# Two attention layers and three feed-forward blocks on one core: order of VectorE in the sparse attention, 14 tokens fewer in two projections, half-width level products

## Chip, cores and metric

The kernel runs on 1 core of one Trainium2 chip. The metric is the device time of one execution in microseconds; shown are the median and the extremes of 3 runs. "Profile" is one further execution, taken by the hardware profiler. A core has TensorE (PE in the rows; its weight loads are PEld), VectorE (DVE), ScalarE (ACT), GpSimd (POOL) and SyncE (SP).

## The reference, cut to what matters

One sequence of 512 tokens, 1024 wide, in float32, goes through two blocks. Three pieces concern the change.

```python
# first block: 16 meta tokens stand ahead of the 512 (528 tokens)
q_a, k_a, v_a, f_a, q_b, k_b, v_b, g_a, g_b = split(rms_norm(h) @ w_in)
mixed = (sigmoid(g_a) * y_a + sigmoid(g_b) * y_b) @ w_out
...
return h[:, N_META:]
# second block, gated linear attention (GLA, 4 heads of 128), per chunk of 64 tokens
decay = exp(where(causal, b[t] - b[s], -inf))     # b: cumulative sum of the log gates
scores = einsum('bhtd,bhsd,bhtsd->bhts', q, k, decay)
# second block, sparse attention (8 heads of 128, blocks of 128 queries)
_, sel = top_k(score, 128)                        # by an indexer
logits = q . kv_sel * dc ** -0.5 + bias           # masked where not selected
probs = softmax(logits)
out = probs @ kv_sel
```

After the first block's attention the kernel keeps only 514 of the 528 tokens: the convolution of width 3 that follows looks two tokens back, and the 16 meta tokens are dropped at the end.

## The kernel before, in words

**The whole.** Activations lie transposed in SBUF (features on the partitions, tokens along the free dimension). Every weight is streamed once from HBM in units of 128x2048 (`raw`); ScalarE rounds a unit to a short float (`whi`, cast at L718, or in quarters at L730), GpSimd subtracts for the rest (`wlo`, L655), and TensorE makes three products for each tile: `whi` by the activations' high part, `whi` by their low part, `wlo` by their high part (`tile_products`, L2197). The order of work on each engine is written out by hand, engine by engine, and semaphores tie the engines together; nothing is scheduled by a planner.

**Projections of the first block.** A chunk is 128 output features by 528 tokens, 8 input tiles of 3 products, each in two pieces of 256 and 272 tokens (`wide_places`): 48 matmuls. The second queries (`q_b`, 4 chunks), second keys (4 chunks) and gates (16 chunks) are interleaved with the attention steps by `dense`. VectorE takes a finished chunk out of PSUM times the inverse root (`scaled`, L1511, L1513). The gates go through a sigmoid on ScalarE (L951) and VectorE reads 514 of their tokens (L1721, L1722). `SKIP` is 14. The corner queries (`corner_queries`) read tokens 512 to 527 of the second queries.

**GLA.** For each head there are 9 kinds of item (`GI`), 36 items in all: kind 0 is the diagonal product, kinds 1 to 7 are levels, kind 8 is what crosses the four 128-token tiles. At level L a tile of 128 tokens is cut into groups of 2^L; the product between the first and the second half of a group is needed. VectorE subtracts (`gf` at L1982, L1983), ScalarE exponentiates, VectorE multiplies (L1992, L1993), TensorE multiplies each 128-token tile of `gf` by itself (L2845, 128 columns for each of 4 tiles, in plain float32, two passes each, so that 8 matmuls stand in the profile), and VectorE copies under a mask of bytes into `sd` (L2016, 512 elements). TensorE fills in with tiles of a projection (`gr_tiles`, L2197).

**Sparse attention.** 32 items, of (block, head): 16 that alternate between blocks 3 and 0 (512 and 128 keys wide), then 16 that alternate between blocks 2 and 1 (384 and 256). Item n goes this way:

- TensorE: scores into a bank (L2929), plus the mask (L2930).
- VectorE: adds the bias and takes the minimum in one instruction (the "minimum", L2087, into `dl`; the logits have their sign turned).
- ScalarE: exponential with the sum (L1294).
- VectorE: reciprocal of the sum and scaling (L2094, L2096, the "normalisation").
- TensorE: transposes into PSUM (L2945).
- ScalarE: copies out (`dpt`, L1290).
- TensorE: the product with the values (L2955).
- ScalarE: high part (`x2hi`, L1283). VectorE: low part (`x2lo`, L2103).

In step n of their loops TensorE does scores n, transposes n-2 and value product n-3; ScalarE does the high part n-4, copy n-2 and exponential n; VectorE does minimum n, normalisation n-1 and low part n-4. TensorE waits for the normalisation (`da_norm`) before the transposes, and for the low part two items back (`da_lo`) before the value product. In steps 8 to 11 ScalarE also casts a quarter of a weight unit (L730).

Of the kernel before, what the change touches and what calls it, by code (L numbers as in the profile page):

```python
# [27 lines left out]
ALU = mybir.AluOpType  # L28
# [3 lines left out]
P = 128  # L32
# [167 lines left out]
def build(nc, wstream, h0, fw, cvec, alpha_w, rel_bias, p2, ident_c, masks_c, gmask_c, onehot_c, out):  # L200
    n_units = wstream.shape[0]
    with ExitStack() as ctx:
# [214 lines left out]

        def diag_seen(q):

            return sum(1 for x in range(q + 1) if GI[x][1] < 8)  # L420
# [49 lines left out]
        U_LAST += [T_GATES + 2 * KC * (i + 1) for i in range(8)]  # L470

# [237 lines left out]
        def _(act):  # L709
# [235 lines left out]
            for m in range(8):  # L945
                if m % 2 == 1:
                    hi_of(U_O + m // 2 + 2)
                if m == 0:
                    act.wait_ge(sig("evac"), D_END)
                for c in (m, 8 + m):  # L950
                    nc.scalar.activation(gates[:, c, :], gates[:, c, :], ACT.Sigmoid).then_inc(sig("gate_on"), 1)  # L951
                act.wait_ge(sig("y_sum"), m + 1)
                nc.scalar.copy(yhi[:, m, :], yt[2 * (m % 2)][:]).then_inc(sig("y_hi"), 1)
# [416 lines left out]
        def _(dve):  # L1370
# [133 lines left out]
            def wide(d):  # L1504

                return regions[:, STAGE1[d][0] // 2, LO:LO + T1]

            def scaled(d, dst, scale=None):

                if scale is None:  # L1510
                    vec.tensor_tensor(dst, wide(d), rt[:], ALU.mult).then_inc(sig("evac"), 1)  # L1511
                else:
                    vec.scalar_tensor_tensor(out=dst, in0=wide(d), scalar=scale, in1=rt[:], op0=ALU.mult,  # L1513
                                             op1=ALU.mult).then_inc(sig("evac"), 1)
# [63 lines left out]
            scaled(7, qkf[:, 6, :])  # L1578
            dve.wait_ge(sig("unit_done"), 4)
# [388 lines left out]
            def halves(ap, L):  # L1968
                v = ap.rearrange("p (n c) -> p n c", c=2 ** L)
                return v[:, :, 0:2 ** (L - 1)], v[:, :, 2 ** (L - 1):]  # L1970

            for q in range(NG + 2):
# [30 lines left out]
                if 0 <= m < NG:  # L2003
# [8 lines left out]
                    elif kind < 8:  # L2012
                        dve.wait_ge(sig("g_cp"), diag_seen(m) - 1)
                        mk = ga_m[:, (kind - 1) * P:kind * P] if kind < 5 else gb_m[:, (kind - 5) * P:(kind - 4) * P]
                        mk = mk.rearrange("p (a c) -> p a c", a=1).to_broadcast([P, 4, P])
                        vec.copy_predicated(sd[hd % 2][:], mk, src).then_inc(sig("g_cp"), 1)  # L2016
# [63 lines left out]
            for n in range(ND + 4):  # L2080
                if n < ND:
                    j, hd = DI[n]
                    w = P * (j + 1)
                    dve.wait_ge(sig("da_s"), n + 1)
                    if n >= 3:
                        dve.wait_ge(sig("da_t"), n - 2)
                    vec.tensor_tensor_reduce(dl[n % 3][:, 0:w], bank(n % 4)[:, 0:w], bias[:, hd, w - 1::-1], 1.0, 3e38,  # L2087
                                             ALU.add, ALU.min, dst_[:, 0, n:n + 1]).then_inc(sig("da_max"), 1)
# [10 lines left out]
                if 0 <= m < ND:  # L2099
# [4 lines left out]
                                      ALU.subtract).then_inc(sig("da_lo"), 1)  # L2104

# [82 lines left out]
        def _(pe):  # L2188
# [65 lines left out]
            def chunk_tile(u, c, k, banks):  # L2254

                return tile_products(u % 2, 2 * k + c, wide_places(banks), lambda tok: xhi[:, k, tok],
                                     lambda tok: xlo[:, k, tok], k == 0, k == KC - 1)
# [88 lines left out]
            def dense(first, last):  # L2346

                for t in range(first, last):
# [10 lines left out]
                    ins = chunk_tile(u, c % 2, k, STAGE1[d])  # L2359
# [462 lines left out]
            for q in range(1, NG + 4):  # L2822
# [9 lines left out]
                if 0 <= m < NG:  # L2832
# [3 lines left out]
                    if kind < 8:  # L2836
                        if m >= 3 and (seen := diag_seen(m - 3)):
                            pe.wait_ge(sig("g_cp"), seen)
                        for j in range(4):
# [3 lines left out]
                            else:  # L2843
                                left = right = gf[m % 3][:, tile]
                            ins = mm(bank(m % 3)[:, tile], left, right, start=True, stop=True)  # L2845
# [230 lines left out]
```

## Time and profile before

| what | value |
|---|---|
| median of 3 runs | 2203.33 us (2202.96 to 2203.38) |
| time of the profiled execution | 2203.01 us |
| its span, first to last instruction | 2201.1 us |
| TensorE busy | 2159.8 us (98%) |
| VectorE, ScalarE, GpSimd busy | 992.3, 753.4, 1005.0 us |
| mean granted TensorE clock | 0.997 |
| DMA, mean over the span | 89 GB/s |

Busy times of TensorE come from modelled ends, and consecutive matmuls overlap in them; the distance from one start to the next says more than a duration. A bracket in a row gives the idle time of the engine before it and what ended it.

### The profile page before, as it was taken

The numbers are of one execution on the slowest core, as the hardware profiler recorded it, in microseconds if no ns is written. First come the engines' busy times: TensorE is split into PE (matmuls) and PEld (weight loads), VectorE is DVE, ScalarE is ACT, GpSimd is POOL, SyncE is SP. The second block draws the span as 40 slices with busy tenths as digits, with TensorE's granted clock in tenths as the row PEclk, the third lists the DMA queues.
The fourth block names the chain that finished last, engine by engine and source line by source line (L and its number), as shares of the span: only waits on it lengthen the run. The fifth ranks groups of instructions, "written<-read, shape, count | busy, mean of one in ns | idle before, by whom it ended". The sixth has DMA issues, their size and how long they took to land.

```text
span 2201.1 us, 31220 instructions
## 1 busy us (share of the span) xinstructions
PE 2159.8 (98%) x12448; PEld 1856.6 (84%) x12448; DVE 992.3 (45%) x1447; ACT 753.4 (34%) x1003; POOL 1005.0 (46%) x812
## 2 busy tenths in 40 slices
PE   8999999989999999999999999999999999999998
PEld 7897999989999887888888787878777888888886
DVE  5144454279888208322201619661875452322017
ACT  4133454343222216322213324551336332222134
POOL 4322223455555547555544543254331555555444
PEclk9999999999999999999999999999999999999999
DMA  4321111212222223222222321024220223222222
GB/s 163 101 72 64 58 59 59 97 58 96 95 94 82 111 100 111 104 95 95 95 99 93 103 93 59 22 75 140 90 77 20 85 90 112 90 101 95 96 97 95
DMA packets 31837, 194.94 MB, mean 89 GB/s; under 512 B 3968, under 2 KB 4480, under 8 KB 9984
## 3 DMA queue, kind: packets, MB, share of 16 engines
q1 hardware_dynamic: 26352, 182.66, 23.3%
q10 hardware_dynamic: 5392, 10.95, 1.6%
q8 instruction: 68, 1.11, 0.2%
q14 instruction: 25, 0.20, 0.0%
HBM read 189.24 MB, written 4.23 MB: 88 GB/s over the span
## 4 chain that ended last, share of the span: by engine, by line
PE 81%; issue 7%; DVE 5%; POOL 4%; ACT 1%; DMA 0%; SPq 0%; DVEq 0%; POOLq 0%; ACTq 0%
PE ps L2197 71%; POOL wlo L655 4%; PE ps L2747 2%; DVE sqa L1428 1%; PE ps L2955 1%; PE ps L2872 1%; PE ps L2929 1%; DVE x2lo L1416 1%; PE ps L2845 1%; ACT whi L718 1%; PE ps L2476 0%; PE ps L2499 0%; PE ps L2910 0%; PE ps L2535 0%; DVE sd L2016 0%
## 5 line engine op out<-in xcount | busy, mean ns | idle before, releaser
L655 POOL TENSOR_TENSOR wlo<-raw,whi 128x512 fp32r<-128x512 f32 (+2 forms) x808 | 1004.7, 1276 | 1172.9 <-ACT whi L718 1081.5
L718 ACT CAST whi<-raw 128x2048 fp32r<-128x2048 f32 x165 | 315.3, 1911 | 825.2 <-PE ps L2197 767.4
L2197 PE MATMUL ps<-x2hi,whi 128*128 128x512 f32 x1136 | 450.8, 397 | 1.3 <-DVE x2lo L1416 1.1
L2197 PE MATMUL ps<-x2hi,wlo 128*128 128x512 f32 x1136 | 442.9, 390 | 0.0
L2197 PE MATMUL ps<-x2lo,whi 128*128 128x512 f32 x1136 | 442.8, 390 | 0.0
L2197 PE MATMUL ps<-xhi,whi 128*128 128x256 f32 x1344 | 276.6, 287 | 20.7 <-DVE xlo L1481 9.5
L2197 PE MATMUL ps<-xlo,whi 128*128 128x256 f32 x1344 | 273.6, 285 | 0.0
L2197 PE MATMUL ps<-xhi,wlo 128*128 128x256 f32 x1344 | 273.4, 285 | 0.0
L2197 PEld LDWEIGHTS ps<-x2hi,whi 128*128 128x128 f32 x1136 | 213.7, 188 | 50.5 <-issue 7.1
L2197 PEld LDWEIGHTS ps<-x2lo,whi 128*128 128x128 f32 x1136 | 213.8, 188 | 45.3 <-issue 2.6
L2197 PEld LDWEIGHTS ps<-x2hi,wlo 128*128 128x128 f32 x1136 | 213.6, 188 | 44.7
L2197 PEld LDWEIGHTS ps<-xhi,whi 128*128 128x128 f32 x1344 | 210.9, 191 | 22.7 <-POOL wlo L655 13.5
L2197 PEld LDWEIGHTS ps<-xlo,whi 128*128 128x128 f32 x1344 | 211.0, 191 | 0.0
L2197 PEld LDWEIGHTS ps<-xhi,wlo 128*128 128x128 f32 x1344 | 210.9, 191 | 0.0
L2197 PE MATMUL ps<-hhi,whi 128*128 (+1 forms) x528 | 205.4, 389 | 0.0
L2197 PE MATMUL ps<-hlo,whi 128*128 (+1 forms) x528 | 205.4, 389 | 0.0
L2197 PE MATMUL ps<-hhi,wlo 128*128 (+1 forms) x528 | 205.4, 389 | 0.0
L2197 PEld LDWEIGHTS ps<-hhi,whi 128*128 128x128 f32 x528 | 99.1, 188 | 20.6
L2197 PEld LDWEIGHTS ps<-hhi,wlo 128*128 128x128 f32 x528 | 99.1, 188 | 20.6
L2197 PEld LDWEIGHTS ps<-hlo,whi 128*128 128x128 f32 x528 | 99.1, 188 | 20.4
L1440 DVE TENSOR_TENSOR cvl<-ps,fold 128x1024 f32<-128x1024 f32 x22 | 26.9, 1224 | 189.3 <-PE ps L2197 189.3
L1878 DVE SCALAR_TENSOR_TENSOR h<-ps,h 128x512 f32<-128x512 f32 x16 | 10.9, 681 | 209.7 <-PE ps L2197 209.7
(439 smaller groups left out, 2747.4 us busy)
## 6 DMA issues: line engine op xcount, KB each, us to landing
raw<-wstream SPq DMA_DIRECT2D x170, 1024.0 KB, 4.8
h<-h SPq DMA_DIRECT2D x4, 528.0 KB, 8.5
ncb<-c_rows ACTq DMA_DIRECT2D x8, 256.0 KB, 3.4
ple_rows<-ple_out ACTq DMA_DIRECT2D x4, 512.0 KB, 3.9
bias<-bias_rows ACTq DMA_DIRECT2D x8, 256.0 KB, 4.6
ple<-ple_rows ACTq DMA_DIRECT2D x4, 512.0 KB, 5.6
out_dram<-outb SPq DMA_DIRECT2D x8, 256.0 KB, 2.9
raw<-wstream ACTq DMA_DIRECT2D x4, 256.0 KB, 7.2
```

What stands on the lines that cost most here:

```text
L655: return nc.gpsimd.tensor_tensor(wlo[b][:, cols], raw[b][:, cols], whi[b][:, cols].bitcast(F32), ALU.subtract)
L718: nc.scalar.copy(whi[b][:], raw[b][:]).then_inc(sig("hi_done"), 1)
L1416: vec.scalar_tensor_tensor(out=xl[:, k, 0:T], in0=view(k), scalar=cv[:, gain + k:gain + k + 1], in1=xh[:, k, 0:T].bitcast(F32), op0=ALU.mu ...
L1428: vec.tensor_tensor(squared[:, 0, :], squared[:, 0, :], squared[:, k, :], ALU.add).then_inc(sig("sq_added"), 1)
L1440: return vec.tensor_tensor(dst, pair(src), scale, ALU.mult)
L1878: vec.scalar_tensor_tensor(out=hview(m), in0=bank(m), scalar=0.5, in1=hview(m), op0=ALU.mult, op1=ALU.add).then_inc(sig("down_evac"), 1)
L2197: ins = mm(dst, w[slot][:, cols], xx(tok), start=first and p_ == 0, stop=last and p_ == 2, skip_group_check=True)
L2747: ins = mm(gv_bank(half, j), xx[:, k if first else k + 4, tok], ww[u % 2][:, cols], start=(first and k == 0 and p_ == 0), stop=(not first ...
L2845: ins = mm(bank(m % 3)[:, tile], left, right, start=True, stop=True)
L2872: ins = mm(dst[:, t_ * P:(t_ + 1) * P], gvt[:, s_, vc], rhs, start=(x_ == 0), stop=(x_ == len(plan) - 1), skip_group_check=True)
L2929: mm(dst, dq[:, hd, j * P:(j + 1) * P], ckvf[:, 0:w], start=True, stop=False)
L2955: ins = mm(bank(6 + m % 2)[:, 0:P], ckvt[:, b, :], dpt[m % 2][:, b * P:(b + 1) * P], start=(b == 0), stop=(b == j))
```

## The change

Three parts.

1. **514 tokens.** The second queries' 4 chunks and the 16 gate chunks leave out the first 14 tokens: the pieces are 256 and 258 instead of 256 and 272 (`first_of`). VectorE's `scaled` and ScalarE's sigmoid work on 514. A `memset` on VectorE sets the second queries' first 14 tokens to zero.
2. **Level products' later halves.** For kinds 1 to 7 the moving operand is only the second half of each group: 64 columns for each tile instead of 128, written side by side in PSUM, and the masked copy covers 256 elements instead of 512, with strides on the mask and the destination.
3. **Order in the sparse attention.** In VectorE's step n the minimum n moves from the front of the step to its end, behind normalisation n-1 and low part n-4.

```diff
+        def halves(ap, L):
+            v = ap.rearrange("p (n c) -> p n c", c=2 ** L)
+            return v[:, :, 0:2 ** (L - 1)], v[:, :, 2 ** (L - 1):]
+
+        def late_of(m, kind):
+            late = bank(m % 3)[:, 0:4 * P // 2]
+            return late.rearrange("p (j n c) -> p j n c", j=4, c=2 ** (kind - 1))
...
+        def first_of(d):
+            return SKIP if D_QKB <= d < D_QKB + 4 or d >= D_GATES else 0
...
-                    nc.scalar.activation(gates[:, c, :], gates[:, c, :], ACT.Sigmoid).then_inc(sig("gate_on"), 1)
+                    used = gates[:, c, SKIP:T1]
+                    nc.scalar.activation(used, used, ACT.Sigmoid).then_inc(sig("gate_on"), 1)
...
             def scaled(d, dst, scale=None):
 
+                dst, roots_ = dst[:, first_of(d):], rt[:, first_of(d):]
...
+            step.up(vec.memset(qkb[:, 0:4, 0:SKIP], 0.0))
...
-                        mk = mk.rearrange("p (a c) -> p a c", a=1).to_broadcast([P, 4, P])
-                        vec.copy_predicated(sd[hd % 2][:], mk, src).then_inc(sig("g_cp"), 1)
+                        n, b = P >> kind, 2 ** (kind - 1)
+                        dst = sd[hd % 2][:].rearrange("p j (n c) -> p j n c", c=2 * b)[:, :, :, b:]
+                        mk = mk.rearrange("p (a n c) -> p a n c", a=1, c=2 * b)[:, :, :, b:].to_broadcast([P, 4, n, b])
+                        vec.copy_predicated(dst, mk, late_of(m, kind)).then_inc(sig("g_cp"), 1)
...
             for n in range(ND + 4):
-                if n < ND:
-                    j, hd = DI[n]
-                    w = P * (j + 1)
-                    dve.wait_ge(sig("da_s"), n + 1)
-                    if n >= 3:
-                        dve.wait_ge(sig("da_t"), n - 2)
-                    vec.tensor_tensor_reduce(dl[n % 3][:, 0:w], bank(n % 4)[:, 0:w], bias[:, hd, w - 1::-1], 1.0, 3e38,
-                                             ALU.add, ALU.min, dst_[:, 0, n:n + 1]).then_inc(sig("da_max"), 1)
                 m = n - 1
...
+                if n < ND:
+                    j, hd = DI[n]
+                    w = P * (j + 1)
+                    dve.wait_ge(sig("da_s"), n + 1)
+                    if n >= 3:
+                        dve.wait_ge(sig("da_t"), n - 2)
+                    vec.tensor_tensor_reduce(dl[n % 3][:, 0:w], bank(n % 4)[:, 0:w], bias[:, hd, w - 1::-1], 1.0, 3e38,
+                                             ALU.add, ALU.min, dst_[:, 0, n:n + 1]).then_inc(sig("da_max"), 1)
...
                 r, cut = regions[:, banks[0] // 2, :], first_token + HALF
                 return [(r[:, LO:BANK], slice(first_token, cut)), (r[:, BANK:BANK + T1 - cut], slice(cut, T1))]
...
-                    ins = chunk_tile(u, c % 2, k, STAGE1[d])
+                    ins = chunk_tile(u, c % 2, k, STAGE1[d], first_of(d))
...
-                                left = right = gf[m % 3][:, tile]
-                            ins = mm(bank(m % 3)[:, tile], left, right, start=True, stop=True)
+                                left, right = gf[m % 3][:, tile], halves(gf[m % 3][:, tile], kind)[1]
+                            dst = bank(m % 3)[:, tile] if kind == 0 else late_of(m, kind)[:, j]
+                            ins = mm(dst, left, right, start=True, stop=True)
```

VectorE's own order in the sparse attention, steady part of the wide and narrow items. ISA is the minimum (the second ISA row reads its result), RECIPROCAL and TENSOR_SCALAR are the normalisation, TENSOR_TENSOR is the low part; `dl_206` to `dl_208` are the three buffers of `dl`. Before:

```order
L2087 ISA dl_208,dst<-ps,bias 128x512 [waits da_t,da_s]
L2087 ISA dst 128x1
L2094 RECIPROCAL dst<-dst 128x1 [waits da_max,da_exp]
L2096 TENSOR_SCALAR dl_207<-dl_207,dst 128x128 [waits dve_step]
L2103 TENSOR_TENSOR x2lo<-ps,x2hi 128x128 [waits da_hi]
L2087 ISA dl_206,dst<-ps,bias 128x128 [waits da_t,da_s]
```

Each minimum is followed by the normalisation of the item before it, in another buffer. With the change:

```order
L2117 ISA dl_208,dst<-ps,bias 128x128 [waits da_t,da_s]
L2117 ISA dst 128x1
L2100 RECIPROCAL dst<-dst 128x1 [waits da_max,da_exp]
L2102 TENSOR_SCALAR dl_208<-dl_208,dst 128x128 [waits dve_step]
L2109 TENSOR_TENSOR x2lo<-ps,x2hi 128x128 [waits da_hi]
L2117 ISA dl_206,dst<-ps,bias 128x512 [waits da_t,da_s]
```

Each minimum is now followed by the normalisation of the same item, in the same buffer, and the next minimum stands behind that.

The level products on TensorE, in the first head of GLA. Before:

```order
L2845 MATMUL ps<-gqk 128x128 x4
L2845 MATMUL ps<-gf_179 128x128 x4
L2197 MATMUL ps<-x2hi,whi_51 128x512
```

With the change:

```order
L2860 MATMUL ps<-gqk 128x128 x4
L2860 MATMUL ps<-gf_179 128x64 x4
L2211 MATMUL ps<-x2hi,whi_51 128x512
```

The number of matmuls and their order stay; a level's matmuls have 64 columns.

## Rows read from the trace of the kernel before

**Rows 1.** Windows: length, busy us (count) by engine, clock; GLA, then sparse attention.

```profile
1343.60:1363.00 19.40, 17.23 (x114) 14.09 (x115) 18.88 (x43) 10.32 (x27) 10.04 (x16) 1.00 0.19 73
1667.52:1689.67 22.15, 22.13 (x147) 18.42 (x146) 16.12 (x71) 15.64 (x55) 0.44 (x1) 1.00 0.13 49
```

**Rows 2.** Timeline (start, duration), sparse attention, one pair of 512 and 128.

```profile
1649.96 0.69 DVE L2087 CUSTOM_DVE_ANT_0 dl<-ps,bias 128x512 f32<-128x512 f32 x1 [1.05 <-PE ps L2930]
...
1650.77 0.29 DVE L2096 TENSOR_SCALAR dl<-dl,dst 128x128 f32<-128x128 f32 x1
1650.88 0.72 ACT L1294 ACTIVATE dl<-dl,dst 128x512 f32<-128x512 f32 x1
1650.98 0.28 DVE L2103 TENSOR_TENSOR x2lo<-ps,x2hi 128x128 fp32r<-128x128 f32 x1
...
1651.11 0.33 PE L2945 MATMUL ps<-ident,dl 128*128 128x128 f32 x1 [0.24 <-DVE dl L2096]
1651.18 0.28 DVE L2087 CUSTOM_DVE_ANT_0 dl<-ps,bias 128x128 f32<-128x128 f32 x1
...
1651.51 0.19 ACT L1294 ACTIVATION_READ_ACCUMULATOR dl<-dl,dst 128x1 f32 x1
...
1651.73 0.16 DVE L2094 RECIPROCAL dst<-dst 128x1 f32<-128x1 f32 x1 [0.27 <-ACT dl L1294]
...
1651.90 0.42 ACT L1294 ACTIVATE dl<-dl,dst 128x128 f32<-128x128 f32 x1
1651.93 0.48 DVE L2096 TENSOR_SCALAR dl<-dl,dst 128x512 f32<-128x512 f32 x1
...
1652.33 0.28 DVE L2103 TENSOR_TENSOR x2lo<-ps,x2hi 128x128 fp32r<-128x128 f32 x1
...
1653.66 0.69 DVE L2087 CUSTOM_DVE_ANT_0 dl<-ps,bias 128x512 f32<-128x512 f32 x1 [1.05 <-PE ps L2930]
```

**Rows 3.** Timeline, sparse attention, the first minimum and its exponential.

```profile
1635.96 0.69 DVE L2087 CUSTOM_DVE_ANT_0 dl<-ps,bias 128x512 f32<-128x512 f32 x1 [2.75 <-PE ps L2930]
...
1636.75 0.73 ACT L1294 ACTIVATE dl<-dl,dst 128x512 f32<-128x512 f32 x1
```

**Rows 4.** Timeline, sparse attention, a weight cast on ScalarE; minimum and exponential of 384.

```profile
1655.30 0.61 ACT L730 CAST whi<-raw 128x512 fp32r<-128x512 f32 x1
...
1681.26 0.56 DVE L2087 CUSTOM_DVE_ANT_0 dl<-ps,bias 128x384 f32<-128x384 f32 x1 [0.66 <-PE ps L2930]
...
1681.96 0.62 ACT L1294 ACTIVATE dl<-dl,dst 128x384 f32<-128x384 f32 x1
```

**Rows 5.** Timeline, sparse attention: third minimum; last reciprocal; next stage's first matmul.

```profile
1642.76 0.69 DVE L2087 CUSTOM_DVE_ANT_0 dl<-ps,bias 128x512 f32<-128x512 f32 x1 [3.02 <-PE ps L2930]
...
1693.16 0.16 DVE L2094 RECIPROCAL dst<-dst 128x1 f32<-128x1 f32 x1
...
1695.29 0.48 PE L2197 MATMUL ps<-x2hi,whi 128*128 128x512 f32 x1
```

**Rows 6.** Timeline of TensorE, GLA, first head, a level that waits and two matmuls ahead.

```profile
1350.70 0.39 PE L2197 MATMUL ps<-x2lo,whi 128*128 128x512 f32 x1
1350.93 0.40 PE L2197 MATMUL ps<-x2hi,wlo 128*128 128x512 f32 x1
1352.29 1.16 PE L2845 MATMUL ps<-gf 128*128 128x128 f32 x8 [0.96 <-DVE gf L1993]
```

**Rows 7.** Groups by line and shape, GLA, VectorE: count, busy us, mean ns.

```profile
L2016 DVE COPY_PREDICATED sd<-ga_m,ps 128x512 f32<-128x512 int8 x16 | 11.6, 724 | 10.3 <-PE ps L2845 10.3
L1982 DVE TENSOR_TENSOR gf<-nbt 128x256 f32<-128x256 f32 x24 | 10.0, 417 | 1.8 <-PE ps L2852 1.8
```

**Rows 8.** Timeline of TensorE, end of the program: plain float32 with one moving column.

```profile
2190.89 1.05 PE L3006 MATMUL ps<-per,sq 128*128 128x1 f32 x8
```

**Rows 9.** Chain that ended last: a gate chunk of 528; output projections of 514.

```profile
293.32 5.91 PE ps L2197 x48
...
358.89 89.89 PE ps L2197 x744
```

More of the change, by code:

```diff
@@ L1504, in wide @@
             def wide(d):
-                return regions[:, STAGE1[d][0] // 2, LO:LO + T1]
+                return regions[:, STAGE1[d][0] // 2, LO:LO + T1 - first_of(d)]
             def scaled(d, dst, scale=None):
+                dst, roots_ = dst[:, first_of(d):], rt[:, first_of(d):]
                 if scale is None:
-                    vec.tensor_tensor(dst, wide(d), rt[:], ALU.mult).then_inc(sig("evac"), 1)
+                    vec.tensor_tensor(dst, wide(d), roots_, ALU.mult).then_inc(sig("evac"), 1)
                 else:
-                    vec.scalar_tensor_tensor(out=dst, in0=wide(d), scalar=scale, in1=rt[:], op0=ALU.mult,
+                    vec.scalar_tensor_tensor(out=dst, in0=wide(d), scalar=scale, in1=roots_, op0=ALU.mult,
                                              op1=ALU.mult).then_inc(sig("evac"), 1)
@@ L1966, in _ @@
                               ).then_inc(sig("nb_ready"), 1)
-            def halves(ap, L):
-                v = ap.rearrange("p (n c) -> p n c", c=2 ** L)
-                return v[:, :, 0:2 ** (L - 1)], v[:, :, 2 ** (L - 1):]
             for q in range(NG + 2):
@@ L2252, in wide_places, with chunk_tile @@
                 return [(r[:, LO:BANK], slice(first_token, cut)), (r[:, BANK:BANK + T1 - cut], slice(cut, T1))]
-            def chunk_tile(u, c, k, banks):
-                return tile_products(u % 2, 2 * k + c, wide_places(banks), lambda tok: xhi[:, k, tok],
+            def chunk_tile(u, c, k, banks, first_token=0):
+                return tile_products(u % 2, 2 * k + c, wide_places(banks, first_token), lambda tok: xhi[:, k, tok],
                                      lambda tok: xlo[:, k, tok], k == 0, k == KC - 1)
```

## The prediction

> **What bounds the kernel now.** I read the page first: TensorE is busy for 98% of the span (the table above), so a change counts where TensorE works without a pause, or where it pauses for another engine. Then the windows of the two stages that the change touches. In the first head of GLA, VectorE is busy for 18.88 of 19.40 us and TensorE has pauses: VectorE sets the pace there. In the second half of the sparse attention (widths 384 and 256) TensorE is busy for 22.13 of 22.15 us [rows 1]. In the first half (512 and 128) a pair of items takes 3.70 us, from one wide minimum to the next; TensorE's transposes wait 0.24 us in each pair for a normalisation, while VectorE itself sits idle for 1.05 us ahead of the wide minimum [rows 2]. Projections run without pauses [rows 9].
>
> The sums below are made against the profiled execution, 2203.01 us with a span of 2201.1; the median of the runs is 0.3 us above it, and I add the sum to the median. A measurement of this kernel can tell about 0.2% (4.4 us) from no change; the chances use that bound.
>
> **514 tokens.** 20 chunks lose 14 columns in 24 of their 48 matmuls. A gate chunk of 528 takes 5.91 us for 48 matmuls, 123.1 ns each; the output projections of 514, part of which also start at token 14, take 89.89 us for 744, 120.8 ns each [rows 9]. That is 2.3 x 48 = 0.11 us in a chunk and 2.2 us in 20 chunks. TensorE sets the end there, so all of it counts. Bounds: 0 (a start at an odd place costs what the columns save) and 3.2 us (14 columns of 20 x 24 matmuls at 120.8 / 257 = 0.47 ns a column). I take 2.2. VectorE's shorter evacuations, the shorter sigmoids and the memset lie beside TensorE's work and count as nothing; if that cover were gone, the memset would cost under 0.2 us.
>
> **Level products.** 28 groups of eight matmuls go from 128 to 64 moving columns. Does the group get shorter? Eight plain float32 matmuls with a single moving column still take 1.05 us [rows 8], and eight with 128 columns 1.16 [rows 6]. The distance between them is thus not set by the columns, and I count nothing for seven of the eight. The last one's columns are not hidden behind another weight load: 64 columns fewer there are up to 0.05 us in a group, 28 x 0.05 = 1.4 us, of which I take 1.0, since some groups end in a wait on VectorE anyway.
>
> The masked copy covers 256 elements instead of 512. It takes 724 ns; a two-operand instruction of 256 elements takes 417 [rows 7]. I take 0.45 us for the new copy, 0.27 less. This counts only where TensorE waits for VectorE. At the level that waits longest, the start of the matmuls comes 1.36 us after that of the matmul ahead, where 0.23 is usual (1350.70 to 1350.93): 1.1 us lost [rows 6]. Two smaller losses of 0.2 and 0.3 lie before it in the same head. Three copies lie ahead of that point in a row of VectorE's instructions without idle time, so 0.8 us comes back there. In the other heads VectorE has idle time, and the loss that can come back is what one to three copies ahead of a wait give; from the starts I count five such places (0.3, 0.3, 0.5, 0.3, 0.3). Together 2.5 us. The waits at the change of head stay, because there VectorE waits for TensorE first. Bounds: 0 (strided copies no faster) and 4. The two terms of this part: 3.5 us, bounds 0 and 5.5.
>
> **The order in the sparse attention.** What it removes: the wide minimum no longer stands ahead of the narrow item's normalisation. What it adds is a wait: normalisation n-1 waits for exponential n-1 on ScalarE, which waits for minimum n-1, and now minimum n is queued behind it. Before, minimum n ran while ScalarE was at exponential n-1. Now VectorE has nothing to do meanwhile, and all items form one chain: minimum, exponential, reciprocal, scaling, low part, next minimum. Its length for one item of 512:
>
> - start of the minimum to start of the exponential: 0.79 us [rows 3];
> - exponential to the end of its sum's read: 1651.51 + 0.19 - 1650.88 = 0.82; to the reciprocal 0.03; to the scaling 0.20; to the low part 0.40 [rows 2];
> - low part to the next minimum: 1651.18 - 1650.98 = 0.20 [rows 2].
>
> Sum 2.44 us. For 128: minimum 0.28 and about 0.07 to the exponential, 0.42 + 0.10, 0.03, 0.20, 0.21, 0.20 [rows 2]: 1.5 us. A pair takes 3.9 us instead of 3.70. For 384 and 256: 0.56 + 0.10 + 0.62 + 0.10 + 0.03 + 0.20 + 0.32 + 0.20 = 2.1, and 0.43 + 0.05 + 0.52 + 0.10 + 0.03 + 0.20 + 0.27 + 0.20 = 1.8 [rows 4], with steps of the widths that have no row put between those that have: 3.9 us again. There TensorE now gets through a pair in about 3.15 us without a pause (22.15 us for seven pairs [rows 1]), so most of the loss lies in the half that has no waits today.
>
> The end: the third minimum starts at 1642.76, behind scores that side work of TensorE holds back in both orders [rows 5]. From there 30 items are 15 pairs, 58.5 us; the last reciprocal comes 0.7 us before their end (scaling, low part and a step), at 1642.8 + 57.8 = 1700.6 instead of 1693.16: 7.4 us later. ScalarE's four casts of 0.61 us [rows 4] stand between exponentials and now delay the high part for which the low part in the chain waits; by the same steps that is 0.1 us for a wide item and 0.3 for a narrow one, twice each: 0.8 us. Behind the last reciprocal TensorE has a value product less to do, 0.2 us. Sum: **8.0 us longer**. Bounds: 6.5 (the quarters hidden, steps 2% shorter) and 10.
>
> **Sum.** -2.2 - 3.5 + 8.0 = +2.3 us: 2203.33 + 2.3 = 2205.6 us, within 0.2%.
>
> **Rivals.**
>
> *The level halves give nothing, and the chain stands alone (slower).* The mechanism: a masked copy whose runs are 1, 2 or 4 elements goes at the pace of the words it passes over, not of those it copies, so that 256 strided elements cost what 512 did. For it: no row has a masked copy with a stride. Against it: the subtractions L1982 have the same strides and take 417 ns on average over the levels [rows 7]. Then the sum is -2.2 + 8.0 and, with the last matmul's 1.0, +4.8 us: 2208.1, over the bound. It decides from a new copy of about 0.65 us on. The Trainium skill (SBUF — State Buffer, "Door 1: The DMA port swizzle") says that each access that crosses to a new 16-byte line pays a penalty; by that rule level 1 would pass over as many lines as before and gain little, the levels from 3 on would gain in full. Chance 0.25.
>
> *The matmuls do get shorter.* If the distance went with the columns, each of 224 matmuls would save 0.055 us, 12 us in all; VectorE has 18.88 of 19.40 us of work in the first head, less 1.9 for seven copies, so at most half can show: another -6 us, 2199.6 us. Against it: the single-column matmuls [rows 8]. The Trainium skill (TensorE: Matmul & The Clock Gate, "Back-to-back issue gap") gives N / 2.4 + 2.5 ns for an isolated matmul, which is this rival's rule; by its "LDWEIGHTS" section, 107 ns for 128 weight columns, the distance would stay, and the one-column row agrees with the latter. Chance 0.1.
>
> *The new order helps (faster).* If the exponential were early enough, each wide pair would lose its pauses: 3.70 us with 0.24 in the row, at most 0.6 us with the wait for the low part behind it, times 7 pairs: 4 us saved instead of 8 lost, 2203.33 - 2.2 - 3.5 - 4 = 2193.6. For it: VectorE is idle for 1.05 us ahead of the wide minimum, and normalising the narrow item would fit in there. Against it: the narrow minimum pays for it, since it now stands behind the wide exponential (0.82 us), with a reciprocal that already waits 0.27 us for ScalarE today [rows 2]. Chance 0.08.
>
> **How the numbers follow.** The forecast case has 0.57, the rivals 0.25, 0.1 and 0.08. In the forecast case the bounds of the terms reach 4.4 us in about a quarter of it, and the slow rival crosses that bound in most of its chance: slower 0.3. Faster: the last rival and a little of the one before, 0.1. The rest, 0.6, is within 0.2%. Range: from 2199.0, which takes in the shorter matmuls, to 2211.5, which takes in the slow rival with the chain at its upper bound of 10 us (514 tokens -1, chain +10, level products -1); only the rival with the helpful order lies wholly outside.
>
> **What the profile of the changed kernel would show.** Right: gate chunks of 48 matmuls in 5.80 us; level groups as long as before; masked copies near 0.45 us; in the sparse attention VectorE idle ahead of every reciprocal until the exponential ends, a pair every 3.9 us in both halves, TensorE with pauses in the second half, and the next stage's first matmul 8 us later than the stage's start alone explains. Wrong: a pair of 384 and 256 still in 3.15 us, or VectorE's wait ahead of the minimum still for TensorE's mask product. A level group of eight in 0.6 us would make the second rival right, a masked copy of 0.65 us or more the first.

## The result, and the profile after

The changed kernel takes 2208.86 us (median of 9 executions, 2207.16 to 2216.11) against 2203.33 us before (2202.92 to 2204.18 in the same comparison). The ratio is 1.0031, with a 95% interval of 1.0023 to 1.0040: slower, by 5.5 us. That lies inside the range given (2199.0 to 2211.5), but the forecast was 2205.6 and its likeliest case "within 0.2%"; the interval lies wholly beyond 0.2%, an outcome to which the prediction gave 0.3.

| what | before | after |
|---|---|---|
| median | 2203.33 us | 2208.86 us |
| profiled execution | 2203.01 us | 2207.16 us |
| its span | 2201.1 us | 2205.3 us |
| TensorE busy | 2159.8 us | 2158.5 us |
| VectorE busy | 992.3 us | 987.3 us |
| mean granted clock, profile | 0.997 | 0.997 |
| mean granted clock, all executions | 0.994 to 0.997 (77 of the later comparisons) | 0.991 to 0.997 |

The profiled execution is the fastest of the nine, 4.15 us above that of before. The other eight reach up to 9 us higher, most of them at a lower mean clock. Both are looked at below.

**Where the 4.15 us come from.** I laid the two profiles side by side and followed the start of the same TensorE matmul in both:

| place (time in before) | after minus before |
|---|---|
| end of the first block's first projections, 380 | -2.4 us |
| a sum of squares in the feed-forward, 873 | -2.8 us |
| GLA, last head, 1414 | -5.6 us |
| end of the selection, 1618 | -4.3 us |
| third item of the sparse attention, 1642.8 | -4.2 us |
| first matmul behind it, 1695.29 | +3.4 us |
| a sum of squares near the end, 2156 | +4.1 us |
| end of the span | +4.2 us |

*Projections.* The chain of waits shows the gate chunk at 5.81 us, 0.10 less than in [rows 9]. In that chain a long stretch of the output projections stays at the old pace, 87.31 us for 726 matmuls, 120.3 ns each:

```profile
281.36 5.81 PE ps L2211 x48
...
358.93 87.31 PE ps L2211 x726
```

*GLA.* TensorE's timeline, first head, the groups that stand ahead of a projection tile:

```profile
1344.60 1.10 PE L2860 MATMUL ps<-gf 128*128 128x64 f32 x8
1345.51 0.48 PE L2211 MATMUL ps<-x2hi,whi 128*128 128x512 f32 x1
...
1347.94 0.40 PE L2211 MATMUL ps<-x2hi,wlo 128*128 128x512 f32 x1
1348.18 1.09 PE L2860 MATMUL ps<-gf 128*128 128x64 f32 x8
1349.08 0.48 PE L2211 MATMUL ps<-x2hi,whi 128*128 128x512 f32 x1
```

Two things are to be seen. The level that waited 0.96 us for VectorE in [rows 6] (now at 1348.18) waits no more; its start comes 0.24 us after the matmul ahead. And that group of eight is hardly shorter for its 64 columns. From its start to the start of the projection matmul behind it there are 0.90 us (1348.18 to 1349.08), against 0.91 before with 128 columns (1352.29 to 1353.20). Some groups take 0.81 us; they do in both kernels.

VectorE's masked copies of the same head, levels 1, 2, 3 and 5:

```profile
1342.57 0.73 DVE L2030 COPY_PREDICATED sd<-ga_m,ps 128x256 f32<-128x256 int8 x1
...
1344.46 0.73 DVE L2030 COPY_PREDICATED sd<-ga_m,ps 128x256 f32<-128x256 int8 x1
...
1346.35 0.43 DVE L2030 COPY_PREDICATED sd<-ga_m,ps 128x256 f32<-128x256 int8 x1
...
1349.31 0.45 DVE L2030 COPY_PREDICATED sd<-gb_m,ps 128x256 f32<-128x256 int8 x1 [0.20 <-PE ps L2860]
```

Levels 1 and 2, whose runs are 1 and 2 elements, take 0.73 us for 256 elements, what 512 took in [rows 7]. From level 3 on (runs of 4 and more) it is 0.43 to 0.45 in this head, 0.42 to 0.46 over all four. The other heads repeat this. VectorE's products ahead of the matmuls go over the same runs of float32 numbers, 256 elements too, and take 0.42 us at every level. This is one of level 1:

```profile
1339.95 0.43 DVE L2004 TENSOR_TENSOR gf<-gf,gqk 128x256 f32<-128x256 f32 x1
```

*Two places that give back.* Of 5.6 us, 1.3 are given back between GLA and the sparse attention, in the selection of keys (0.1 more just behind it), and 0.7 near 2156. TensorE's timeline has a wait at each that before has not:

```profile
1613.88 0.50 PE L2211 MATMUL ps<-x2hi,whi 128*128 128x512 f32 x1 [1.13 <-POOL wlo L668]
...
2160.38 1.12 PE L2254 MATMUL ps<-sqa,per 128*128 128x512 f32 x2 [0.83 <-DVE sqa L1442]
```

Both begin on VectorE, with pauses of 0.46 to 0.48 us for which no releaser is late; its timeline after:

```profile
1544.19 0.75 DVE L2077 SCALAR_TENSOR_TENSOR acc<-rl,per,acc 128x512 f32<-128x512 f32 x1
1545.41 1.61 DVE L2077 SCALAR_TENSOR_TENSOR acc<-rl,per,acc 128x512 f32<-128x512 f32 x2 [0.47 <-ACT rl L1284]
...
1605.21 0.35 DVE L2074 TENSOR_SCALAR acc<-rl,per 128x256 f32<-128x256 f32 x1 [0.46 <-DVE mj L2089]
...
2156.89 3.43 DVE L1442 TENSOR_TENSOR sqa<-sqa 128x512 f32<-128x512 f32 x4 [0.48 <-DVE sqa L1442]
```

ScalarE, which is named in the first bracket, had ended the result in question (its third of eight) 0.96 us before, and in the kernel before these accumulations run one behind the other. There is a third such pause, of 0.46 us at 1605.21, also in the selection; it lies on the same chain. In the selection the pauses have a consequence. GpSimd's low part of a weight hangs on a cast of ScalarE, which stands behind `rl`, which waits for VectorE's accumulation of scores. This is how VectorE and GpSimd stood before:

```profile
1585.03 0.62 DVE L2063 SCALAR_TENSOR_TENSOR acc<-rl,per,acc 128x384 f32<-128x384 f32 x1
...
1585.39 2.97 POOL L655 TENSOR_TENSOR wlo<-raw,whi 128x512 fp32r<-128x512 f32 x2 [9.57 <-ACT whi L718]
...
1585.75 1.46 DVE L2063 SCALAR_TENSOR_TENSOR acc<-rl,per,acc 128x384 f32<-128x384 f32 x1
```

After:

```profile
1579.03 0.62 DVE L2077 SCALAR_TENSOR_TENSOR acc<-rl,per,acc 128x384 f32<-128x384 f32 x1
...
1579.75 1.73 DVE L2077 SCALAR_TENSOR_TENSOR acc<-rl,per,acc 128x384 f32<-128x384 f32 x1
1579.77 4.42 POOL L668 TENSOR_TENSOR wlo<-raw,whi 128x512 fp32r<-128x512 f32 x3 [9.57 <-ACT whi L731]
```

The same accumulation of 384 elements takes 0.62 us by itself and 1.46 or 1.73 us beside GpSimd's subtraction. Against GpSimd VectorE stands 0.3 us later than before, so that one more of them falls beside the subtraction: 1.1 us on VectorE's chain. With 0.35 us for each of the two pauses (a distance of 0.1 us stands between two instructions anyway) VectorE is 1.8 us later at the end of this chain, the cast and GpSimd's low part behind it are as well, and TensorE loses 1.3 us.

*Sparse attention.* VectorE's timeline, the steady part of the first half, one pair:

```profile
1646.20 0.68 DVE L2117 CUSTOM_DVE_ANT_0 dl<-ps,bias 128x512 f32<-128x512 f32 x1
...
1647.77 0.16 DVE L2100 RECIPROCAL dst<-dst 128x1 f32<-128x1 f32 x1 [0.88 <-ACT dl L1308]
1647.97 0.48 DVE L2102 TENSOR_SCALAR dl<-dl,dst 128x512 f32<-128x512 f32 x1
1648.37 0.28 DVE L2109 TENSOR_TENSOR x2lo<-ps,x2hi 128x128 fp32r<-128x128 f32 x1
1648.57 0.28 DVE L2117 CUSTOM_DVE_ANT_0 dl<-ps,bias 128x128 f32<-128x128 f32 x1
...
1649.42 0.16 DVE L2100 RECIPROCAL dst<-dst 128x1 f32<-128x1 f32 x1 [0.56 <-ACT dl L1308]
...
1650.03 0.68 DVE L2117 CUSTOM_DVE_ANT_0 dl<-ps,bias 128x512 f32<-128x512 f32 x1
```

VectorE is idle ahead of every reciprocal until the exponential of the same item ends; ahead of the minima it waits for nothing, where before it waited 1.05 us for TensorE [rows 2]. A pair takes 3.83 us (3.70 before). In the second half, all engines, one pair:

```profile
1678.17 0.44 PE L2960 MATMUL ps<-ident,dl 128*128 128x128 f32 x2 [0.22 <-DVE dl L2102]
1678.22 0.55 DVE L2117 CUSTOM_DVE_ANT_0 dl<-ps,bias 128x384 f32<-128x384 f32 x1
...
1678.81 0.61 ACT L1308 ACTIVATE dl<-dl,dst 128x384 f32<-128x384 f32 x1 [0.76 <-DVE dst L2117]
...
1679.55 0.17 DVE L2100 RECIPROCAL dst<-dst 128x1 f32<-128x1 f32 x1 [0.77 <-ACT dl L1308]
...
1681.38 0.16 DVE L2100 RECIPROCAL dst<-dst 128x1 f32<-128x1 f32 x1 [0.67 <-ACT dl L1308]
...
1681.99 0.44 PE L2960 MATMUL ps<-ident,dl 128*128 128x128 f32 x2 [0.21 <-DVE dl L2102]
1682.05 0.55 DVE L2117 CUSTOM_DVE_ANT_0 dl<-ps,bias 128x384 f32<-128x384 f32 x1
```

Again 3.83 us a pair, where TensorE without a pause needed 3.15. From the third item (-4.2) to the matmul behind this stage (+3.4) that is 7.6 us. ScalarE and VectorE now take turns, and TensorE, 22.13 of 22.15 us busy in [rows 1], waits for the normalisation.

### The profile page after: what moved, and what is told of

It reads as the page before. It is cut to its first block, busy times and chain, and to the rows that moved or that the text cites. A ratio compares the mean times of both kernels' runs of the same rounds, so it can differ in the third digit from the quotient of the medians.

```text
span 2205.3 us, 31221 instructions
## 1 busy us (share of the span) xinstructions
PE 2158.5 (98%) x12448; PEld 1852.3 (84%) x12448; DVE 987.3 (45%) x1448; ACT 753.4 (34%) x1003; POOL 1005.6 (46%) x812
## 4 chain that ended last, share of the span: by engine, by line
PE 74%; issue 12%; POOL 6%; DVE 5%; ACT 2%; DMA 0%; POOLq 0%; SPq 0%; DVEq 0%; ACTq 0%
PE ps L2211 66%; POOL wlo L668 6%; PE ps L2761 2%; PE ps L2860 1%; DVE sqa L1442 1%; PE ps L2887 1%; DVE x2lo L1430 1%; DVE dl L2117 1%; ACT whi L731 1%; PE ps L2490 0%; PE ps L2513 0%; PE ps L2549 0%; DMA h<-h 0%; DVE nbt L1978 0%; ACT dl L1308 0%
```

## The experiments

Theory of the first four runs: the order costs some 8 us by the chain of minimum, exponential and normalisation, and the 64-column matmuls go with the falls of the clock. The rival for the order: the loss hangs on the other two parts, which bring the stage earlier. The rival for the clock: it falls by itself or with the pauses of the sparse attention. "Before" has 24 executions beside them, median 2203.37 us (2202.95 to 2205.02).

**The order alone.** Before, with the block of the minimum moved behind the low part, as in the change:

```diff
             for n in range(ND + 4):
-                if n < ND:
-                    ...
-                    vec.tensor_tensor_reduce(dl[n % 3][:, 0:w], ...
                 m = n - 1
...
+                if n < ND:
+                    ...
+                    vec.tensor_tensor_reduce(dl[n % 3][:, 0:w], ...
```

> The kernel before with the new order of VectorE in the sparse attention alone. Theory (one chain through VectorE and ScalarE): the stage gets 8 us longer at full clock, so about 2203.3 + 8 = 2211.3 us, and a pair of 384 and 256 takes 3.8 to 3.9 us. The changed kernel showed a granted clock between 0.991 and 0.997 over its executions, where its profiled one had 0.997; if the short pauses of TensorE in this stage are what lowers it, this kernel shows the same spread, with executions up to 9 us above its fastest. Rival (the stage lost less and the level halves gave nothing): 2203.3 + 5 or less.

Measured: 2211.58 us (2210.84 to 2212.92, 5 executions), 1.0037 (1.0024 to 1.0050). By the profile the sparse attention is 7.6 us longer (the program 7.9), everything else as before. Every execution has a mean clock of 0.996. So the chain costs nearly its 8 us without the other parts, and its pauses don't lower the clock.

**The change without the order.** The changed kernel, with the minimum back at the front of the step.

> The changed kernel with the old order of VectorE in the sparse attention (514 tokens and level halves stay). Theory: at the end of GLA it is 5.5 us ahead of the kernel before, as the changed kernel was; 1 to 2 us of that is given back in the indexer's selection, so 2203.3 - 4 = 2199.3 us, with a clock of 0.997 in every execution. Rival (what is ahead at the end of GLA is lost in full in the selection, whose chain on VectorE sets the pace): 2203 us. Rival for the clock (the lower clock has nothing to do with the order): executions at 0.991 to 0.995 here too.

Measured: 2202.8 us (2200.11 to 2208.13, 11 executions), 1.0000 (0.9992 to 1.0009). The fastest execution is 2.8 us under the fastest of before; the clock goes down to 0.992, and four of the eleven are above 2206 us. The two other parts gain about 3 us where the clock holds, and the clock takes that away in the median. The clock expected, 0.997 in every execution, did not come; the rival did: the spread is there without the order.

**The new order only where it can help.** In the first half, ahead of the wide minimum only: there VectorE is idle for 1.05 us [rows 2], while the narrow minimum would pay for it.

```diff
+                narrow_first = n < ND // 2 and n % 2 == 0
+                for part in ((norm_low, minimum) if narrow_first else (minimum, norm_low)):
+                    part()
```

> As no_order, but in the first half of the sparse attention (512 and 128) normalisation and low part go ahead of the minimum where the minimum is the wide one, and stay behind it where it is the narrow one; the second half keeps the old order. Theory: the narrow item's exponential is long done when the wide minimum waits for its scores, so the move costs nothing and takes TensorE's wait of 0.24 us and the one behind it away: 0.3 to 0.5 us a pair, 2 to 3.5 us less than no_order, about 2196.5. Rival (any normalisation ahead of a minimum lengthens the loop): as no_order or slower.

Measured: 2201.12 us (2197.85 to 2204.81, 11 executions), 0.9987 (0.9978 to 0.9996); the fastest is 2.3 us under that of the run without the order. VectorE's timeline of one pair:

```profile
1643.44 0.69 DVE L2102 CUSTOM_DVE_ANT_0 dl<-ps,bias 128x512 f32<-128x512 f32 x1 [0.32 <-PE ps L2950]
...
1644.39 0.29 DVE L2102 CUSTOM_DVE_ANT_0 dl<-ps,bias 128x128 f32<-128x128 f32 x1 [0.25 <-PE ps L2950]
...
1645.21 0.16 DVE L2110 RECIPROCAL dst<-dst 128x1 f32<-128x1 f32 x1 [0.52 <-ACT dl L1308]
...
1646.01 0.15 DVE L2110 RECIPROCAL dst<-dst 128x1 f32<-128x1 f32 x1
...
1646.81 0.69 DVE L2102 CUSTOM_DVE_ANT_0 dl<-ps,bias 128x512 f32<-128x512 f32 x1
```

The two minima stand together, then the two normalisations, and a pair takes 3.37 us instead of 3.70. TensorE has no wait left in this pair. Against the run without the order TensorE gains 2.1 us in this stage. The median is above the 2196.5 us expected, with clocks down to 0.992.

**The changed kernel again,** beside these three.

> The changed kernel once more, for its spread on this chip. Theory: fastest at 2207, clocks between 0.991 and 0.997 and times that go with them (some 9 us between the ends). Rival (the spread was one chip's): all at 2207 with 0.997.

Measured: 2208.27 us (2207.38 to 2216.0, 7 executions), 1.0031 (1.0018 to 1.0043). Both executions at 2216.0 have a mean clock of 0.991, the other five 0.994 to 0.997.

The next four runs take the other two parts apart and test the clock. "Before" has 32 executions beside them, median 2204.14 us.

**The level halves alone.**

> The kernel before with the level products' later halves alone (64-column matmuls and copies of 256 elements; 528 tokens and the old order stay). Theory: 3.1 us less at the end of GLA, about 1.3 of it given back in the indexer, so fastest executions near 2201.5 us. On the clock, theory A: the 64-column matmuls leave TensorE with less done in GLA, and the clock goes down there in some executions, so this kernel shows clocks of 0.991 to 0.995 and a spread of several us, as no_order and the changed kernel did, while before and order_only kept to 0.994 to 0.997. Theory B: the spread comes with the 514 tokens; then this kernel keeps within 2 us.

Measured: 2201.53 us (2200.15 to 2208.84, 11 executions), 0.9995 (0.9986 to 1.0005), clocks of 0.991 to 0.996. The fastest is 1.3 us under what was expected, because nothing is given back in the selection. Here the profile caught an execution with a low clock, 2206.51 us. Its windows over GLA (length, busy us and count of TensorE, its weight loads, VectorE, ScalarE, GpSimd, granted clock, DMA share, GB/s):

```profile
1340.00:1350.00 10.00, 7.34 (x34) 6.58 (x32) 8.99 (x22) 4.45 (x8) 2.15 (x6) 0.69 0.29 107
1350.00:1360.00 10.00, 10.00 (x40) 9.13 (x39) 6.53 (x14) 4.75 (x16) 6.34 (x12) 0.50 0.25 78
1360.00:1370.00 10.00, 9.30 (x69) 8.61 (x69) 7.92 (x22) 3.18 (x5) 0.00 (x0) 0.96 0.07 29
```

TensorE's timeline in that stretch:

```profile
1349.37 1.80 PE L2859 MATMUL ps<-gf 128*128 128x64 f32 x8
1350.93 0.77 PE L2210 MATMUL ps<-x2hi,whi 128*128 128x512 f32 x1
```

The clock is at its lower level (1.2 GHz) from 1343.8 to 1360.9, and a group takes 1.56 us instead of 0.81 to 0.91 (1349.37 to 1350.93). In the second window TensorE is busy throughout, but gets through 40 matmuls in ten microseconds. Against the run with half the copy, below, it falls 6.6 us behind here (to 1360). Before the clock fell, TensorE had stood still for 2.66 us, waiting for VectorE ahead of its first level group:

```profile
1343.50 1.70 PE L2859 MATMUL ps<-gf 128*128 128x64 f32 x8 [2.66 <-DVE gf L2004]
```

Before has a pause of 2.15 us there, with 128 columns behind it, and no fall. What before has is a low stretch 20 us earlier (1322.8 to 1326.2), and this execution hasn't got that one, which returns 1.7 us of the loss.

**514 tokens alone.**

> The kernel before with 514 tokens alone. Theory: 2.0 us less at the end of the first projections, kept to the end, so 2201.3 us. On the clock, theory A: within 2 us, 0.994 to 0.997. Theory B: spread of several us and 0.991 here.

Measured: 2203.18 us (2202.51 to 2203.8, 11 executions), 0.9997 (0.9988 to 1.0006), clocks 0.995 and 0.996. The 2201.3 us expected did not come. Its TensorE is 2.6 us ahead at 873. It loses 1.6 us of that at 1322, where the clock's low stretch lasts from 1318.2 to 1325.1 instead of 1322.8 to 1326.2, then 1.4 us in the selection and just behind it and 0.7 near 2156: the two waits of the changed kernel stand here too (this is the first), and the three pauses of VectorE.

```profile
1617.86 0.50 PE L2209 MATMUL ps<-x2hi,whi 128*128 128x512 f32 x1 [1.12 <-POOL wlo L668]
```

So what is given back belongs to this part of the change. The next run hasn't got it.

**Half the copy, whole matmuls.** As the level halves alone, but TensorE keeps 128 columns, and the copy reads the later halves with a stride.

```diff
-                                left, right = gf[m % 3][:, tile], halves(gf[m % 3][:, tile], kind)[1]
-                            dst = bank(m % 3)[:, tile] if kind == 0 else late_of(m, kind)[:, j]
-                            ins = mm(dst, left, right, start=True, stop=True)
+                                left = right = gf[m % 3][:, tile]
+                            ins = mm(bank(m % 3)[:, tile], left, right, start=True, stop=True)
```

> As levels_only, but the matmuls keep 128 columns and only the masked copy takes the later halves (256 elements, now read with strides from PSUM too). Theory: the matmuls' distance did not change with 64 columns and the gain was VectorE's, so the same 3 us less at the end of GLA and fastest executions as levels_only. On the clock, theory A: no spread here, 0.994 to 0.997. Rival (strided reading of PSUM costs VectorE what the shorter copy saves): GLA as in the kernel before.

Measured: 2200.61 us (2200.23 to 2202.11, 11 executions), 0.9987 (0.9978 to 0.9996), clocks 0.995 and 0.996. TensorE is 2.7 us earlier at the end of GLA, and the fastest execution is level with that of the 64 columns (2200.15). The copies take 0.72 to 0.73 and 0.42 to 0.46 us here as well, although they now read PSUM with a stride. Taken group by group, 64 columns shorten 6 of the 28 by 0.02 to 0.06 us, 0.3 us in all, of which 0.1 us is left at the end of GLA. So nearly the whole gain is the copy's, and what the 64 columns bring is mostly the spread. The same windows as above:

```profile
1340.00:1350.00 10.00, 7.65 (x50) 6.00 (x49) 9.94 (x26) 5.69 (x10) 2.16 (x3) 1.00 0.28 107
1350.00:1360.00 10.00, 9.16 (x63) 7.82 (x62) 8.95 (x21) 6.09 (x19) 9.23 (x15) 1.00 0.00 0
```

**What works of each part, together:** 514 tokens, half the copy with whole matmuls, and the new order for the wide minima of the first half.

> 514 tokens, the half-width masked copy with 128-column matmuls, and the order of mixed. Theory: the sum of tokens_only, copy_half and mixed's 1.9 us in the sparse attention, about 2198 us, and by theory A with no spread beyond 2 us, so a median under those of mixed (2201.1) and of both kernels. Rival (theory B): a median near 2201 with a spread of 7 us.

Measured: 2198.14 us (2197.85 to 2199.3, 10 executions), 0.9975 (0.9966 to 0.9985), clocks 0.994 to 0.996. It beats before by about 5.5 us (by the ratio) and the changed kernel by about 10. It differs from the mixed order above only in the 128 columns, which the copy reads with a stride: the fastest executions are the same (2197.85), the median is 3.0 us lower and the slowest 5.5 us.

The last three runs ask where the three pauses of VectorE come from, which all kernels with the 514 tokens have at these instructions and no other so far. "Before" has 22 executions beside them, median 2203.64 us.

**One instruction more.** The kernel before, with the memset and nothing else of the change.

```diff
             scaled(7, qkf[:, 6, :])
+            step.up(vec.memset(qkb[:, 0:4, 0:14], 0.0))
```

> The kernel before with one more instruction on VectorE, a memset of the second queries' first 14 tokens at the place where the change has it; no matmul is shorter. In the profiles of all kernels with the 514 tokens VectorE has a pause of 0.47 us ahead of the second accumulation of the selection and one of 0.48 us ahead of a sum of squares near 2153 us, for which no releaser was late; the kernels without the memset have neither. Theory: the pauses and what hangs on them (a wait of TensorE of 1.1 us for GpSimd's low part at 1614 and one of 0.8 us for VectorE near 2157) come from the one additional instruction in VectorE's program. Then this kernel has both pauses and both waits and takes 2203.3 + 1.3 + 0.85 = 2205.5 us. Rival: they come from everything being 2.5 us earlier against weights and GpSimd. Then this kernel has neither and takes 2203.3 us.

Measured: 2205.71 us (2204.51 to 2206.03, 11 executions), 1.0008 (0.9999 to 1.0017). Its profile has the pauses of VectorE at the same three instructions, and both give-backs in about the size expected (+1.3 us in the selection and 0.1 just behind it, +0.7 near 2156):

```profile
1550.57 0.75 DVE L2064 SCALAR_TENSOR_TENSOR acc<-rl,per,acc 128x512 f32<-128x512 f32 x1
1551.79 0.75 DVE L2064 SCALAR_TENSOR_TENSOR acc<-rl,per,acc 128x512 f32<-128x512 f32 x1 [0.47 <-ACT rl L1270]
```

TensorE's wait near the end is there as well:

```profile
2159.16 1.12 PE L2241 MATMUL ps<-sqa,per 128*128 128x512 f32 x2 [0.83 <-DVE sqa L1428]
```

The memset itself, at some 150 us, costs nothing there. The rival, that an earlier start brings the pauses, is out: nothing is earlier here.

And the pauses aren't simply added. Before has one of the same kind at another place, which is gone in the kernels with the one instruction more, where TensorE gains 0.2 us at that point:

```profile
867.95 3.19 DVE L1428 TENSOR_TENSOR sqa<-sqa 128x512 f32<-128x512 f32 x3 [0.47 <-DVE sqa L1428]
```

**As many instructions as before.** The combined kernel, with another memset of VectorE taken out and a column of ones read in its place.

```diff
-            step.up(vec.memset(fz[:], 1.0))
...
-            vec.tensor_tensor_scan(crow[:], fz[:], fm[:], 0.0, ...
+            vec.tensor_tensor_scan(crow[:], small[0:8, 0:1].to_broadcast([8, T1]), fm[:], 0.0, ...
```

> The combined kernel (514 tokens, half copies with whole matmuls, mixed order; 2198.1 us) with one memset of VectorE taken out: the ones for the cumulative sum of the forget gates are read from a column of ones instead, so that VectorE has as many instructions behind that point as before. By the theory (one additional instruction moves the pauses) both pauses and both waits go, and it takes some 2196.0 us. By the rival (the earlier start) they stay, and it takes 2198.1 us.

Measured: 2197.67 us (fastest 2195.91, 10 executions), 0.9972 (0.9962 to 0.9982). The profile caught an execution of 3591.89 us at a mean clock of 0.556, which says nothing of the time. But VectorE's instructions take there what they take elsewhere, and the three pauses are gone: the accumulations run through, while the pause in the feed-forward (0.47 us) is back where before has it.

```profile
2505.36 5.89 DVE L2077 SCALAR_TENSOR_TENSOR acc<-rl,per,acc 128x512 f32<-128x512 f32 x7
```

The fastest execution is 1.9 us under that of the combined kernel (2197.85), as expected; the median is only 0.5 us lower, and the two intervals overlap.

**Two instructions more.** The combined kernel with the memset of the second queries split in two.

> The combined kernel with the memset of the second queries split in two, so that VectorE has two instructions more than before behind that point. By the theory the pauses move by one instruction more against the work: they no longer stand exactly ahead of the second accumulation, and the time changes by up to 2 us in either direction. By the rival nothing changes: 2198.1 us and the pause at the second accumulation stays.

Measured: 2197.62 us (2196.05 to 2197.95, 7 executions), 0.9972 (0.9961 to 0.9983). The three pauses are gone, VectorE's seven accumulations run through, and neither wait of TensorE is there; the span of the profile is 2195.0 us against 2197.3 of the combined kernel, and the fastest execution is 1.8 us lower, though the median again by only 0.5.

```profile
1545.20 0.49 DVE L2076 TENSOR_SCALAR acc<-rl,per 128x512 f32<-128x512 f32 x1 [5.83 <-ACT rl L1284]
1545.80 5.89 DVE L2079 SCALAR_TENSOR_TENSOR acc<-rl,per,acc 128x512 f32<-128x512 f32 x7
```

A pause of VectorE thus stands or falls with the number of instructions ahead of it in its program, not with any wait for data. Counted in the trace's records of VectorE, waits included, it stands ahead of the 1033rd in every kernel with none or two more, and ahead of the 1543rd, 1671st and 2181st in every kernel with one more. In this last run it has moved by one sum of squares against before, a sum and the wait ahead of it being two records. What VectorE does in it the profile doesn't say, nor why one instruction more changes the pattern. That a kernel of two instructions more is as fast as one without any says that it is luck where such a pause falls.

**The clock, over all runs.** Executions with a mean clock of 0.993 or less: with 64 columns 3 of 9 and 2 of 7 (the changed kernel), 4 of 11 (without the order), 4 of 11 (mixed) and 3 of 11 (level halves alone); with 128 columns none of 24, 31 and 22 (before) nor of 5, 11, 11, 10, 11, 9 and 7 (one execution of before and one of the run with as many instructions, over a thousand microseconds off, are left out). Both widths ran on the same chip in the first group of runs (10 of 29 against none of 29) and in the second (3 of 11 against none of 63). One profile shows the place of such a fall; that the others have it there too is inferred from their mean clocks.

## Why the prediction was right and wrong

- **The order, +8.0:** right, and by its mechanism. Measured +7.6 in the stage, alone and in the changed kernel. The chain was put at 3.9 us a pair and is 3.83 in both halves. Beside ScalarE's casts four pairs take 4.13 to 4.25, 1.4 us more in all where the prediction had 0.8; the shorter steps outweigh that. TensorE has pauses in the second half, as said.
- **514 tokens, -2.2:** about -2.0 at the place where it was reckoned (5.91 to 5.81 us a chunk), within the bounds. The step that failed is "if that cover were gone, the memset would cost under 0.2 us". It costs 2.1 us, far from its place: one more instruction in VectorE's program puts three pauses of 0.46 to 0.48 us ahead of instructions on which others hang. That eats the part's whole gain: alone, its ratio of 0.9997 (0.9988 to 1.0006) can't be told from none.
- **Level products, VectorE's part, -2.5:** right in size, -2.7. The copy's 0.45 us holds for five levels of seven. In two it is 0.73, so the slow rival was right for runs of 1 and 2 elements and wrong for those of 4, which it also named. By the line rule cited in the prediction (the Trainium skill, SBUF — State Buffer, "Door 1: The DMA port swizzle") levels 1 and 2 both touch every 16-byte line of four numbers and gain nothing, and from level 3 on half of the lines are left out; the copies' times agree at every level. But the rule is not shown as their cause. That section of the Trainium skill also says that two accesses to a line are enough for full bandwidth, which levels 1 and 2 have; and the products over the same runs take 0.42 us at every level. So it is something of the masked copy, and no run takes its mask and its destination apart. The gain came nevertheless, because the copies ahead of the level that waits are enough.
- **Level products, the last matmul of a group, -1.0:** hardly came. The step that failed is "64 columns fewer there are up to 0.05 us in a group", counted for most groups: 22 of the 28 are as long as with 128 columns (0.81 to 0.91 us), six are 0.02 to 0.06 us shorter, and 0.1 us of that is left at the end of GLA. What sets a group's length no run shows.
- **The matmuls do get shorter** (0.1) is refuted by the same rows; the one-column row had said so [rows 8]. **The new order helps** (0.08) is refuted as the change has it; of what spoke for it, the 1.05 us of idle time, the mixed order draws 2.1 us.
- **What was missing:** besides the 2.1 us of the memset, the clock. In the two profiles of mean clock 0.997 the sum is -2.8 (to 873) - 2.8 (GLA) + 1.4 (selection) + 7.6 (order) + 0.7 (near 2156) = +4.1 us, against +2.3. The forecast without its 1.0 for the last matmuls and with 2.1 for the one instruction would have been +5.4; the order (0.4 less), GLA (0.3 more) and the start of the program (0.4 earlier) make most of the rest. So the total stayed inside the range in part by luck, since these misses have both signs. The median lies 1.7 us above the profiled execution, where before it was 0.3. For 1.1 us of this the changed kernel's second profile (2208.27 us, mean clock 0.995) shows the place: the two low stretches of the clock at 452 and 1319 last 10.3 and 6.8 us instead of 6.9 and 3.4. The falls of the clock in three executions of nine move the median up further. No case of mine had either.

## What to carry to other kernels

Software pipelining between two engines lives from the item that runs ahead: before an instruction is moved in front of the next item's first step, check that what it waits for isn't started by that very item; where items alternate in width, the move may pay for one of the two only. Halving a moving operand shortens next to nothing where eight matmuls take as long with one column as with 128, so measure from start to start. And where a gain of 2 us vanishes, look far behind the edit too: a pause whose named releaser was long done may stand there because of one more instruction, and a variant with one or two idle instructions tells it at once.

## What the runs showed of the hardware that I had not expected

- **Pauses that go with the instruction count.** VectorE stood still for 0.46 to 0.48 us at three fixed instructions in every kernel with one instruction more ahead of them (the profiles of six kernels), and not in those with none (five) or two more (one), which have one such pause at another place. The three cost 2.1 us in the program.
- **Same pace, lower clock.** Plain float32 matmuls with 64 moving columns keep the pace of 128 almost exactly, but in about a third of the executions the mean clock is lower, in the one that was profiled by 17 us at 1.2 GHz in GLA and at a cost of 6.6 us. Of over 140 executions with 128 columns none shows it. Why some executions fall and others don't stays open.
- **VectorE beside GpSimd.** An accumulation with two tensors as inputs (384 elements) takes 0.62 us alone and 1.46 to 1.73 us beside a subtraction of GpSimd. The Trainium skill (SBUF — State Buffer, "Who interferes with whom") says that such an instruction and one of GpSimd that reads SBUF exclude each other, and the second waits for the first; the trace agrees roughly in size, an instruction of GpSimd there taking 1.47 us (4.42 for 3), though VectorE's record starts 0.02 us ahead of GpSimd's.
- **Masked copies with stride.** 256 elements in runs of 1 or 2 take 0.73 us, in runs of 4 to 64 they take 0.42 to 0.46. Products of two tensors over the same runs take 0.42 us at every level.
